# FFN up projection: seven of the 22 slab pairs of each layer computed by seven half-size products

## What is computed

```
D_MODEL, SEQ, D_FF, CONV_WIDTH = 1024, 512, 2816, 3

def conv_ffn(x, w_up, conv_w, conv_b, w_down):
    h = x @ w_up                                   # 1024 -> 5632
    ch = h.shape[-1]
    h = lax.conv_general_dilated(h, conv_w[:, None, :], window_strides=(1,),
                                 padding=((CONV_WIDTH - 1, 0),), ..., feature_group_count=ch) + conv_b
    gate, val = jnp.split(h, 2, axis=-1)
    return (jax.nn.silu(gate) * val) @ w_down

...
        x = x + rms_norm(m, post_mix)
        x = x + rms_norm(conv_ffn(rms_norm(x, pre_ffn), *ffns[i]), post_ffn)
```

## Time and profile before

| | us |
|---|---|
| median of 3 runs | 2073.37 |
| lowest, highest | 2070.84, 2076.74 |
| the profiled execution, its own time | 2073.53 |
| its span in the trace | 2071.8 |
| PE busy | 2053.4 (99%) |
| PE's weight loads busy | 1728.4 (83%) |
| DVE busy | 1413.2 (68%) |
| ACT busy | 1023.9 (49%) |
| POOL busy | 398.3 (19%) |

### The profile page before, as it was taken

One profiled execution on the slowest core, in us unless ns is written; L12 is line 12 of the kernel. 1 busy time (PEld: TensorE's weight loads), 2 busy tenths in 40 slices (PEclk: granted clock), 3 DMA queues, 4 the chain that ended last, 5 costly groups with the idle time before them and its releaser, 6 DMA issues.

```text
span 2071.8 us, 32448 instructions
## 1 busy us (share of the span) xinstructions
PE 2053.4 (99%) x11724; PEld 1728.4 (83%) x11724; DVE 1413.2 (68%) x2250; ACT 1023.9 (49%) x1671; POOL 398.3 (19%) x454
## 2 busy tenths in 40 slices
PE   9999999999999999999999999999999999999998
PEld 8889888888988888888877898888878889888886
DVE  5665555999366555699788655456987666554897
ACT  4754333557334433456556644334565764333555
POOL 0520211310000121120045401212200520121220
PEclk9999999999999999999999999999999999999999
DMA  8123322384430332267421113233674131233383
GB/s 287 63 102 102 100 88 95 120 262 157 143 132 31 102 101 92 90 189 244 156 72 42 62 41 104 99 101 96 193 229 163 63 103 60 87 98 101 105 265 117
DMA packets 73881, 251.62 MB, mean 121 GB/s; under 512 B 8448, under 2 KB 12672, under 8 KB 73392
## 3 DMA queue, kind: packets, MB, share of 16 engines
q1 hardware_dynamic: 58752, 213.10, 31.2%
q0 software_dynamic: 7168, 16.78, 3.7%
q10 hardware_dynamic: 7856, 20.34, 2.8%
HBM read 248.04 MB, written 6.34 MB: 123 GB/s over the span
## 4 chain that ended last, share of the span: by engine, by line
PE 85%; DVE 9%; ACT 2%; DMA 2%; issue 1%; POOL 0%; DVEq 0%; ACTq 0%; SPq 0%; POOLq 0%
PE ps L2011 16%; PE ps L2013 16%; PE ps L2012 16%; PE ps L2196 6%; PE ps L2530 4%; PE ps L2532 4%; PE ps L2531 4%; PE ps L2083 2%; DMA raw<-slabs 2%; DVE w_lo L1352 2%; PE ps L2039 2%; PE ps L2041 2%; PE ps L2040 2%; PE ps L2071 1%; PE ps L2055 1%; PE ps L2056 1%
## 5 line engine op out<-in xcount | busy, mean ns | idle before, releaser
L2011 PE MATMUL ps<-h_hi,w_hi 128*128 128x512 f32 (+1 forms) x1552 | 606.6, 391 | 0.0
L2012 PE MATMUL ps<-h_lo,w_hi 128*128 128x512 f32 (+1 forms) x1552 | 603.2, 389 | 0.0
L2013 PE MATMUL ps<-h_hi,w_lo 128*128 128x512 f32 (+1 forms) x1552 | 603.2, 389 | 0.0
L1747 DVE SCALAR_TENSOR_TENSOR work<-ps,conv_sb,work 128x511 f32<-128x511 f32 (+1 forms) x352 | 246.2, 744 | 379.4 <-ACT work L1138 379.2
L1352 DVE TENSOR_TENSOR w_lo<-raw,w_hi 128x1024 fp32r<-128x1024 f32 x356 | 439.1, 1240 | 43.6 <-ACT w_hi L777 39.9
L777 ACT ACTIVATE w_hi<-raw 128x1024 fp32r<-128x1024 f32 x368 | 384.5, 1051 | 129.9 <-DVE raw L1836 71.8
L1138 ACT ACTIVATE work<-ps,conv_sb 128x512 f32<-128x512 f32 x176 | 137.0, 778 | 474.7 <-PE ps L2013 445.5
L2011 PEld LDWEIGHTS ps<-h_hi,w_hi 128*128 128x128 f32 x1552 | 291.4, 188 | 62.6 <-issue 4.0
L2013 PEld LDWEIGHTS ps<-h_hi,w_lo 128*128 128x128 f32 x1552 | 291.3, 188 | 60.5
L2012 PEld LDWEIGHTS ps<-h_lo,w_hi 128*128 128x128 f32 x1552 | 291.5, 188 | 58.6
L718 POOL TENSOR_TENSOR bias<-act 128x256 f32<-128x256 f32 x40 | 78.7, 1967 | 996.4 <-DVE act L1753 996.4
(11 more groups left out here) (289 smaller groups left out, 3367.5 us busy)
## 6 DMA issues: line engine op xcount, KB each, us to landing
raw<-slabs SPq DMA_DIRECT2D x368, 512.0 KB, 3.8
act<-slabs POOLq DMA_DIRECT2D x64, 256.0 KB, 5.5
bias<-slabs SPq DMA_DIRECT2D x16, 512.0 KB, 6.1
act<-slabs SPq DMA_DIRECT2D x12, 512.0 KB, 5.7
bias_dram<-bias_rows ACTq DMA_DIRECT2D x2, 2048.0 KB, 13.3
g_post<-gains ACTq DMA_DIRECT2D x8, 512.0 KB, 4.9
bias<-bias_dram ACTq DMA_DIRECT2D x2, 2048.0 KB, 9.6
g_pre<-gains ACTq DMA_DIRECT2D x7, 512.0 KB, 6.9
```

The costliest lines, as they stand in the source:

```text
L1747: ve.scalar_tensor_tensor(y, ps[:, 2 * par + e, 0:SEQ - sh], conv_sb[:, L, t, tap:tap + 1], y, ALU.mult, ALU.add).then_inc(done, 1)
L2011: pe.matmul(ps[:, bank, cols], hi, h_hi[:, k, cols], start=k == 0, stop=False)
L2012: pe.matmul(ps[:, bank, cols], hi, h_lo[:, k, cols], start=False, stop=False)
L2013: last = pe.matmul(ps[:, bank, cols], lo, h_hi[:, k, cols], start=False, stop=k == KT - 1)
```

## The change

The even pairs q = 4, 6, ..., 16 of each layer (`FAST`, `FAST_END`; 7 pairs, 28 in all) are computed by seven products in place of eight; call them fast pairs. The pair of slabs is a 2x2 matrix of halves (slab by input half, each 128 channels by 512 inputs), the input a 2x2 matrix of quarters (input half by token half, 512 by 256). Each product is 4 input blocks by 3 matmuls with 256 moving columns: 12 matmuls, 84 for the pair. PE takes them as: 1 `a11`, 2 `a12`, 3 `x2`, 4 `x1`, 5 `x3`, then the first slab of the ordinary pair q+1, 6 `a22`, 7 `x4`, then the second slab of pair q+1. Products 3, 5 and 6 are added onto the bank quarter that product 1 wrote.

- Weights: DVE makes four sums of half slabs (`x1`, `x2`, `x3_x4`, 128x512 each). ACT and DVE split five parts instead of two slabs (`part_hi`, `part_lo`: `a11` and `x1` of 1024 columns, `x2`, `x3`, `x4` of 512).
- Outputs: ACT copies the growing quarter out three times (`copy`, 128x256, from PSUM), DVE adds the copies back in PSUM (`c11`, `c22`, `c12`, 128x256). The gate slab comes out with its sign turned, which the negated taps `conv_neg` undo.
- Input, once a layer: DVE joins h_hi and h_lo to four whole quarters (`join`), makes four differences (`differ`), and ACT and DVE split these (`in_high`, `in_low`), all of 1024 columns. They stand in `g_post`, `g_pre`, two rows of `work` and all of `x`.
- `x` is therefore written to DRAM by four DMAs at the start of the stage and read back by four after pair 17, all issued by ACT. The norm after the down projection waits for that (`x_back`).
- The loads of a fast pair wait for the parts made of the fast pair before (`x1`, `x2`, `x3`; for its second slab `x3` and `x4`), and SP's queue is in order.
- The hardware loops of this stage are gone; the orders of ACT and DVE are written out as `period(q)`.

```
+                def copy(q, n):
...
+                        sc.wait_ge(up_mm, 5 * fast(L, q) + (1, 3)[n])
+                    if q > FAST:
+                        sc.wait_ge(up_c, 3 * fast(L, q - 2) + (1, 3, 2)[n])
+                    sc.activation(kept_sum(n), ps[:, up_bank(q, 0), 0:HALF], ACT.Copy).then_inc(up_copy, 1)
...
+                    tap(1, i - 1, 1)
+                    split_hi(up_slab(L, q + 1))
+                    silu(1, i - 1)
+                    copy(q, 0)
+                    part_hi(q, "x3")
+                    split_hi(up_slab(L, q + 1, 1))
+                    copy(q, 1)
+                    part_hi(q, "x4")
+                    copy(q, 2)
...
+                for t in range(TT):
+                    sc.wait_ge(xn_made, TT * (2 * L + 1) + t + 1)
+                    sc.dma_start(x_dram[t], x[:, t, :]).then_inc(x_out, 16)
...
+                sc.wait_ge(w_used, up_slab(L, FAST_END))
+                for t in range(TT):
+                    sc.dma_start(x[:, t, :], x_dram[t]).then_inc(x_back, 16)
...
+                def product(q, e, half, name, operand, begin, onto=False):
+                    o = ps[:, up_bank(q, e), HALF * half:HALF * (half + 1)]
+                    (hi, lo), (b_hi, b_lo) = up_parts(L, q, name), operand
+                    for k in range(KT // 2):
+                        w = slice(k * P, (k + 1) * P)
+                        pe.matmul(o, hi[:, w], b_hi[:, k, :], start=begin and k == 0, stop=False, skip_group_check=onto)
+                        pe.matmul(o, hi[:, w], b_lo[:, k, :], start=False, stop=False, skip_group_check=onto)
+                        last = pe.matmul(o, lo[:, w], b_hi[:, k, :], start=False, stop=k == KT // 2 - 1, skip_group_check=onto)
+                    return last
...
+                    product(q, 0, 0, "a11", h_quarter(0, 0), True).then_inc(up_mm, 1)
+                    product(q, 1, 0, "a12", h_quarter(1, 0), True).then_inc(up_mm, 1)
+                    pe.wait_ge(up_copy, 3 * f + 1)
+                    pe.wait_ge(part_lo_made["x2"], f + 1)
+                    pe.wait_ge(in_lo, 4 * L + 4)
+                    product(q, 0, 0, "x2", in_parts(2), False, True).then_inc(up_mm, 1)
+                    pe.wait_ge(part_lo_made["x1"], f + 1)
+                    product(q, 1, 1, "x1", in_parts(0), True).then_inc(w_used, 1)
+                    pe.wait_ge(up_copy, 3 * f + 2)
+                    pe.wait_ge(part_lo_made["x3"], f + 1)
+                    product(q, 0, 0, "x3", in_parts(1), False, True).then_inc(w_used, 1)
+                    pe.wait_ge(tap0, UP_SLABS * L + 2 * q)
+                    forward(even + 2, 0, 2)
+                    pe.wait_ge(up_c, 3 * f + 2)
+                    product(q, 0, 0, "a22", in_parts(3), False, True).then_inc(up_mm, 1)
+                    pe.wait_ge(part_lo_made["x4"], f + 1)
+                    product(q, 1, 1, "x4", h_quarter(1, 1), False, True).then_inc(up_mm, 1)
+                    forward(even + 3, 0, 3)
```

More of the change, by code:

```diff
@@ L186, in build @@
         t_made = sem("t_made")
+        neg_made = sem("neg_made")
+        x_out = sem("x_out")
+        x_back = sem("x_back")
+        in_sum = sem("in_sum")
+        in_hi = sem("in_hi")
+        in_lo = sem("in_lo")
+        up_x1 = sem("up_x1")
+        up_x3 = sem("up_x3")
+        up_x4 = sem("up_x4")
+        part_hi_made = {name: sem(f"{name}_hi") for name in PARTS}
+        part_lo_made = {name: sem(f"{name}_lo") for name in PARTS}
+        up_x2 = sem("up_x2")
+        up_mm = sem("up_mm")
+        up_copy = sem("up_copy")
+        up_c = sem("up_c")
         t1_first = sem("t1_first")
@@ L755, in _ @@
                     at_probs(BASE[L])
-                down_sums(L)
+                for j in range(STEPS - 1):
+                    down_sums(L, j)
                 first_sums(L)
@@ L1373, in y @@
                         ve.wait_ge(x_new, p0 + t)
+                    elif k > 0 and k % 2 == 0:
+                        ve.wait_ge(x_back, 8 * TT * k)
                     ve.wait_ge(post_r, p0 + t + 1)
@@ new lines, in c12, with part_lo @@
+                def c12(q):
+                    o = ps[:, up_bank(q, 1), HALF:SEQ]
+                    ve.wait_ge(up_mm, 5 * fast(L, q) + 5)
+                    ve.tensor_tensor(o, o, kept_sum(1), ALU.add).then_inc(up_c, 1)
+                def part_lo(q, name):
+                    hi, lo = part_places(L, q, name)
+                    ve.wait_ge(part_hi_made[name], fast(L, q) + 1)
+                    ve.tensor_tensor(lo, part_source(L, q, name), hi.bitcast(f32), ALU.subtract).then_inc(part_lo_made[name], 1)
@@ L1760, in pair @@
                     split_lo(n0 + 2 * c + 1 + AHEAD, i)
+                if L == 0:
+                    ve.wait_ge(consts_in, 16 * EXTRA)
+                    ve.tensor_scalar(conv_neg[:, :, :, :], conv_sb.rearrange("p l (q e) f -> p l q e f", e=2)[
+                        :, :, FAST:FAST_END:2, 0, 0:3], -1.0, None, ALU.mult).then_inc(neg_made, 1)
                 end = FFT // 2 - 1
[L1763 to L1767, removed]
+                for n in range(4):
+                    join(n)
+                pair(0)
+                differ(0)
+                differ(1)
+                pair(1)
+                differ(2)
+                differ(3)
+                in_low(0)
+                in_low(1)
+                in_low(2)
+                x1(FAST)
+                x2(FAST)
+                taps(0, 1)
+                part_lo(FAST, "x1")
+                gate(0, 1)
+                part_lo(FAST, "a11")
+                in_low(3)
+                part_lo(FAST, "x2")
+                x3_x4(FAST)
+                slab_taps(FAST - 1, 0)
+                for q in range(FAST, FAST_END, 2):
+                    period(q)
+                slab_taps(FAST_END - 1, 1)
+                split_lo(up_slab(L, FAST_END + 1))
+                gate(1, end - 2)
+                split_lo(up_slab(L, FAST_END + 1, 1))
                 pair(0, end - 1)
@@ new lines, in ffn_up @@
+                for c in range(2):
+                    pair(c, 1)
+                for q in range(FAST, FAST_END, 2):
+                    even, f = up_slab(L, q), fast(L, q)
+                    if q >= FAST + 4:
+                        pe.wait_ge(tap0, UP_SLABS * L + 2 * (q - 4) + 2)
+                    pe.wait_ge(part_lo_made["a11"], f + 1)
+                    product(q, 0, 0, "a11", h_quarter(0, 0), True).then_inc(up_mm, 1)
[16 more added lines that the diff above has]
+                    forward(even + 3, 0, 3)
@@ L2523, in ffn_down @@
+                for q in range(FAST_END, FFT):
+                    pe.wait_ge(tap0, UP_SLABS * L + 2 * q - 2)
+                    forward(up_slab(L, q), 0, 2 * (q % 2))
+                    forward(up_slab(L, q, 1), 0, 2 * (q % 2) + 1)
             def ffn_down(L, k):
```

267 lines of the change are left out of this document (242 added, 25 removed).

## The result

The changed kernel takes **2088.9 us** (median of 4, 2087.8 to 2092.1), the kernel before in the same comparison 2072.1 (2070.7 to 2076.7): a ratio of 1.008, 95% interval 1.006 to 1.010. It is slower by 17 us, where 7 us less were forecast, and 3 us outside the range.

The account below looks back on a forecast made before the run. PE's queue, busy for 99% of the span, was taken as the bound. -22.4 + 10 + 3.6 + 1.6 = -7.2 against 2073.53 gave 2066.3, as a median 2066.1 us; range 2057 to 2086 (8 in 10).

Parts of the forecast that it names:

- PE's saving and the steady period: Up stage: each fast pair 0.80 us shorter, 22.4 us off; first copy just late, 0.15 a pair, 3.6 us back.
- The start of the stage: First fast pair of each layer: DVE's added operand work makes PE wait about 2.5 us, 10 us back.
- Loads: Next fast pair's second slab, up stage: its load costs nothing, and begins to cost above 4.5 us.
- rival 4: Fast pairs: the reload is late, 1.4 us past the point where it costs, 34 us on top: 2100 us (7%).
- x out and back: Pair 18: issuing four DMAs on ACT delays the down projection's first operand, 0.4 us a layer, 1.6 us back.
- Rival 2: Fast pairs' chain: GpSimd operations block DVE's, PE waits 0.84 us more a period: 2086 us (20%).
- Rivals 1, 3, 5: Up stage: PE waits less, 2058 (10%); DVE slower throughout, 2073.8 (20%); 256 columns run at 0.113, about 2062 (3%).

Follow-up runs that it names:

- the experiment with the copy ahead: The early reload with ScalarE's copy of the first half product put ahead of the SiLU in each fast period: 2069.5 us, 0.9990 to the kernel before.
- the early reload: The changed kernel with the four DMAs that bring x back issued before pair 18's taps instead of behind them: 2069.1 us, 0.9992 to the kernel before.
- the later start: The early reload with the first fast pair at pair 6 instead of 4 and the operand work spread over more ordinary pairs: 2060.9 us, again 2064.2.
- the late reload: The changed kernel with the four DMAs that bring x back moved into the down stage, behind the copy of the first finished products: 2072.9 us, 1.0008.
- half of it early: The changed kernel with two of the reload's four DMAs ahead of pair 18's taps, two left behind them: 2075.1 us, 1.0015 to the kernel before.

## Why the prediction was wrong

- **PE's saving and the steady period: right in the number.** 256-column matmuls start 0.120 us apart (203.99, 204.11, 204.23 in layer 0), ordinary ones as before. A period takes 21.07 us; the forecast was 20.96 + 0.15 = 21.11. The small delay was forecast for the copy, and in the changed kernel it does stand at product 3: the second matmul comes 0.187 after the first in place of 0.120. But the experiment with the copy ahead shows that the copy isn't the only way by which VectorE sets it. The estimate from the Trainium skill's 109 and 216 ns (TensorE: Matmul & The Clock Gate, on the missing 2.5 ns), which stood beside the sum, saves 1.2 us a pair, 0.4 more than the 0.80 of the rows.
- **The start of the stage: right in place, cause and about in size.** 1.9 us at the first fast pair against 2.5. Not forecast was that the clock may fall after the 1.9: in layer 1 of the changed kernel it did (0.80 and 0.77 in the 8 us from 704), and the tap of slab 11, the last ordinary slab behind the first fast pair, came 55.07 us after the layer's first, against 53.79 in layer 0. With this and the next point the gain to slab 37 was 5.5 us, not the -22.4 + 10 + 3.6 = -8.8 of the sum.
- **Loads: put at nothing, with a limit that was too high.** PE waits for `copy` at three later fast pairs too, 2.5 us in all (10.1 less 4 x 1.9). Behind each stands a late load. The longest, in layer 2: the load (L716, issued at 1388.46) from issue to landing, then VectorE's sum for `x2`, which uses it, then PE's wait for the copy:

```profile
DMA to landing us min/median/max: 5.4/5.4/5.4
```

```profile
1393.94 0.69 DVE L2017 TENSOR_TENSOR act<-raw 128x512 f32<-128x512 f32 x1 [4.41 <-issue]
```

```profile
1405.39 0.39 PE L2874 MATMUL ps<-work_r,a_hi 128*128 128x256 f32 x1 [1.68 <-ACT bias L1265]
```

  The loads of 4.05, 4.21 and 5.40 us gave waits of 0.36, 0.51 and 1.68: always the load less 3.7. The limit is 3.7 us and not the 4.5 of the forecast, and the other loads at this place took 3.1 to 3.4, with VectorE idle for about 2.2 us before the sum where nearly 3 was forecast. The four later waits with the early reload (2.6 us) and the one of 1.3 with the later start follow loads of 4.1 to 5.0 us in the same way. So rival 4, if its "reload" is the load of the next slab into its row, did come true, in 3 places of 24 and for 2.5 us, not for 34.
- **x out and back: the step that failed.** I priced the issue of the four DMAs on ACT and the delay of the first operand behind them, 0.4 us a layer with bounds 0 and 1.4, and noted that `x_back` comes early enough. I asked when the reload is needed, not what it stands in the way of. Measured, in place of 1.6 us: 16.6 us of waiting at VectorE's first sum, 17.8 at PE, 22.8 with the lost clock and the rest. The same transfers in the kernel before cost 18.7. What it took was at hand: four loads in a row take 5.9 us in the median and up to 9.2, the load of down slab 0 was read 3.3 us after its issue in the trace of before, and I had written that VectorE works without a gap there. I worked out a limit for the fast pairs' loads only, none for the down slabs'.
  The Trainium skill (DMA: Bandwidth & Descriptors, on issuing engines not being separate DMA queues) says that DMAs started by different engines run on the same 16 DMA engines and interleave, so that starting them from several engines saves only time on the sequencers. The trace agrees: beside ACT's four transfers SP's load took 7.0 us in place of 3.2. By that rule the slab loads would have been priced as part of one row of six, which is what the term lacked.
- **Rival 2 gave 2086 for another reason.** Its number came nearest, by luck: its mechanism didn't happen in the steady period: GpSimd's sums ran beside VectorE in each period (232.10 to 237.6 in layer 0), and no wait of PE in the steady period follows. At the stage's end of layer 0 four VectorE rows that stand beside them are longer by 2.3 us together, 1.2 more than before. That may be part of the 1.4 us that PE still waits with the early reload, which leaves these sums as they are, and no more.
- **Rivals 1, 3, 5: no.** The period is 0.04 us from the forecast, and 256 columns take 0.120.
- What the change itself is worth, with the reload out of the way, is 0.9992 (0.9983 to 1.0001), nearly nothing. The periods don't say so by themselves: 24 x 0.69 = 16.6 us, less 4 x 1.4 to slab 11 (53.8 against 52.4 before), leaves 11. In its profile the four layers gained 6.4 to slab 37; the late loads take 2.6 of the difference, and the rest is not accounted for. That profile is also of the fastest of its eleven executions (2065.6, mean granted clock 0.999), and in it the clock never fell before the program's end; the slowest two (2073.1 and 2074.4) have means of 0.996 and 0.997.

Left open: what decides whether the clock falls after a wait of 1.9 us (at the first fast pairs it fell once of four in the changed kernel, never in the early reload's profile, twice with the late reload, three times with half of it early), and why single loads are late. For these the traces give something that stands beside them. In the ten kernels with fast pairs, 24 of 224 loads at this place took 3.8 us or more. With 21 of the 24 a transfer of the kind that the profile calls instruction (queue q8, 16 KB) began within 1 us of the issue, and with 6 of the other 200. No run changed that, so it is not shown as the cause.

## What to carry to other kernels

A transfer has a price at the place where it is issued, not only where it is awaited: for each DMA that is added, list the loads that are issued within its landing time, from any queue, and how long after issue each is read. A load that nobody waits for may have no slack at all; read the distance from issue to first use before trusting a wait of zero. When a copy's wait is removed and the time stays, look at what is waited for one step later, and give the engine that is late less to do at that place rather than another order.

## What the runs showed of the hardware

- A load of 512 KB took 3.2 us with no transfer of another queue beside it, 4.3 beside two of another engine's queue, 7.0 beside four. Later issue did not mean later landing: slab 0, issued at 368.70, was there at 375.7, while the last of the reload, issued at 368.2, took 9.1 us and landed at 377.3.
- With each of the 13 waits of 3.9 us and more at the start of a down stage (in the four kernels that have the whole reload behind pair 18's taps) the granted clock went to its lower level, 1.2 GHz, for 3.4 or 6.8 us; after one of 2.99 it did not. After the waits of 1.9 us at the first fast pair it did so in 6 of 16 (changed kernel, early, late and half early reload), and in the changed kernel the next ordinary pair's tap then came 1.3 us later (55.07 against 53.79).
